# Two-direction state-space layer: another order for the last stage of each head group, the norm factor applied behind the last output products, and PSUM copies on ScalarE

## The reference, cut to what matters

```python
def ssd_mixer(u, w_in, conv_w, conv_b, dt_bias, a_log, d_skip, norm_w, w_out):
    proj = u @ w_in
    z = proj[..., :SSD_D_INNER]
    xbc = silu(dwconv_centred(proj[..., SSD_D_INNER:SSD_D_INNER + SSD_CONV_DIM], conv_w, conv_b))
    ...
    dt = softplus(dt_raw + dt_bias)
    y = y_fwd + y_bwd + xh * d_skip
    y = y * silu(z)
    yg = y.reshape(bsz, seq, SSD_GROUPS, SSD_D_INNER // SSD_GROUPS)
    yg = yg * rsqrt(mean(yg * yg, axis=-1, keepdims=True) + NORM_EPS)
    return (yg.reshape(bsz, seq, SSD_D_INNER) * norm_w) @ w_out
```

## Time and profile before

| | us |
|---|---|
| median of 3 runs | 1836.99 (1836.5 to 1837.8) |
| the profiled execution | 1833.54 |
| its span on the core | 1831.8 |
| PE busy in the span | 1578.1 (86%) |
| DVE busy | 1282.2 (70%) |
| ACT busy | 781.0 (43%) |
| POOL busy | 165.6 (9%) |

### The profile page before, as it was taken

How to read it: one execution, slowest core, us unless ns; L and a number is a source line. 1 busy time by engine, 2 the same in 40 slices (tenths; PEclk the granted TensorE clock), 3 DMA queues, 4 the chain that set the end, 5 groups by cost and what they waited for, 6 DMA issues and landing times.

```text
span 1831.8 us, 20798 instructions
## 1 busy us (share of the span) xinstructions
PE 1578.1 (86%) x7275; PEld 1269.4 (69%) x7275; DVE 1282.2 (70%) x1673; ACT 781.0 (43%) x1323; POOL 165.6 (9%) x200
## 2 busy tenths in 40 slices
PE   3984987987985799999998777887898999999996
PEld 1753756755754588778877556887686888888875
DVE  4577766866875676696679898997466677663355
ACT  3348465473473455513442322221234555542242
POOL 1153000000000450000001020000010000000000
PEclk7987998998997899999999986675899999999998
DMA  2233313303320523252334564662232323333231
GB/s 71 82 92 117 92 46 115 105 33 118 112 70 23 114 87 97 81 184 92 102 133 161 191 240 143 162 166 53 66 104 70 102 92 100 95 97 104 90 94 64
DMA packets 189607, 190.57 MB, mean 104 GB/s; under 512 B 47566, under 2 KB 178206, under 8 KB 185438
## 3 DMA queue, kind: packets, MB, share of 16 engines
q1 hardware_dynamic: 168926, 187.52, 32.4%
q10 hardware_dynamic: 20608, 2.10, 0.9%
HBM read 165.27 MB, written 24.31 MB: 103 GB/s over the span
## 4 chain that ended last, share of the span: by engine, by line
PE 59%; DVE 25%; ACT 9%; issue 4%; DMA 2%; ACTq 1%; SPq 1%; DVEq 0%
PE ring L1829 19%; PE ring L1830 18%; PE ring L1831 18%; ACT rows L992 3%; ACT rows L1002 3%; DVE w_lo L1224 2%; DVE rb L1631 2%; DMA rows<-log_decays 1%; DVE ul L1238 1%; PE pe_y L1972 1%; DVE cc L1348 1%; DVE s_prod L1590 1%; DVE tab L1551 1%; DVE ytmp L1502 1%; DVE rstd L1247 1%
## 5 line engine op out<-in xcount | busy, mean ns | idle before, releaser
L879 ACT ACTIVATE w_hi<-w_raw 128x1024 fp32r<-128x1024 f32 (+1 forms) x233 | 239.9, 1029 | 656.7 <-PE ring L1831 626.2
L1829 PE MATMUL ring<-uh,w_hi 128*128 128x512 f32 (+1 forms) x1160 | 461.9, 398 | 36.5 <-DVE w_lo L1224 30.1
L1830 PE MATMUL ring<-ul,w_hi 128*128 128x512 f32 (+1 forms) x1160 | 455.7, 393 | 0.0
L1831 PE MATMUL ring<-uh,w_lo 128*128 128x512 f32 (+1 forms) x1160 | 455.0, 392 | 0.0
L1224 DVE TENSOR_TENSOR w_lo<-w_raw,w_hi 128x1024 fp32r<-128x1024 f32 (+1 forms) x233 | 278.0, 1195 | 188.4 <-ACT w_hi L879 188.2
L1829 PEld LDWEIGHTS ring<-uh,w_hi 128*128 128x128 f32 (+1 forms) x1160 | 220.1, 190 | 94.7 <-DVE w_lo L1224 25.7
L1830 PEld LDWEIGHTS ring<-ul,w_hi 128*128 128x128 f32 (+1 forms) x1160 | 220.1, 190 | 47.3 <-issue 2.1
L1831 PEld LDWEIGHTS ring<-uh,w_lo 128*128 128x128 f32 (+1 forms) x1160 | 219.7, 189 | 47.4 <-issue 0.6
L1829 PE MATMUL ring<-gh,w_hi 128*128 128x512 f32 x480 | 190.5, 397 | 29.2 <-DVE w_lo L1224 16.1
L1830 PE MATMUL ring<-gl,w_hi 128*128 128x512 f32 x480 | 189.1, 394 | 0.0
L1831 PE MATMUL ring<-gh,w_lo 128*128 128x512 f32 x480 | 189.0, 394 | 0.0
(11 more groups left out here) (250 smaller groups left out, 2173.9 us busy)
## 6 DMA issues: line engine op xcount, KB each, us to landing
w_raw<-in_ffn_w_up SPq DMA_DIRECT2D x88, 512.0 KB, 3.5
w_raw<-in_ffn_w_down SPq DMA_DIRECT2D x40, 512.0 KB, 3.5
w_raw<-in_ssd_w_in SPq DMA_DIRECT2D x32, 512.0 KB, 4.4
rows<-log_decays SPq DMA_DIRECT2D x16, 1024.0 KB, 5.9
s_tables<-tab SPq DMA_DIRECT2D x16, 1024.0 KB, 6.2
slot<-s_tables SPq DMA_DIRECT2D x16, 1024.0 KB, 7.4
w_raw<-in_ssd_w_out SPq DMA_DIRECT2D x16, 512.0 KB, 3.5
w_raw<-in_ple_w_gate SPq DMA_DIRECT2D x16, 512.0 KB, 3.5
```

Of the source, the lines that this page charges most:

```text
L879: act.activation(w_hi[u % 2][:, 0:n], w_raw[:, u % 2, 0:n], ACT.Copy).then_inc(hi_done, 1)
L1829: pe.matmul(o, wh[:, k, c], rh[:, k0 + k, :], start=first and k == 0, stop=False)
L1830: pe.matmul(o, wh[:, k, c], rl[:, k0 + k, :], start=False, stop=False)
L1831: mm_ = pe.matmul(o, wl[:, k, c], rh[:, k0 + k, :], start=False, stop=last and k == nk - 1)
```

## The change

- ACT, not DVE, copies `xseq` (four tiles) and `bseq` out of PSUM, right behind the `hi` of the last z unit and ahead of the silu of z.
- PE, y stage: transposes of pairs 0 and 1 first; then per pair outputs, transposes two pairs ahead, and one filler product. In group 0 the fillers are the first two units of the next projection, behind pairs 1 and 3; in groups 1 and 2 the output products 1, 2, 3 of the group before behind pairs 0, 1, 2, and both projection units behind pair 3; in group 3 output products 1, 2 and 3 behind pairs 0, 1 and 3. `group_square` comes behind all that.
- DVE, y stage: add_yoff and weigh of pair 0; then per pair lo, take_out, finish, and add_yoff and weigh of the next pair.
- Last group: y is multiplied by the weight alone, per pair right behind its finish, rounded and its rest made per pair, into memory of its own (`yh_last`, `yl_last`). The norm factor `ytmp` multiplies the output products instead: `take_last_out` has two multiplications into a scratch tile and two additions to `h` where `take_out` had two additions. `group_square` of the last group stands behind its first output product.

```diff
@@ scalar
                 hi_to(z + 3)
+                for c in range(SB + 1):
+                    name, k = (("xseq", g), c) if c < SB else (("bseq", g), 0)
+                    act.wait_ge(evac, T[name] + k)
+                    act.wait_ge(filled, FILL[name] + k + 1)
+                    dst = xseq[:, c, :] if c < SB else bseq[:].rearrange("p c n -> p (c n)")
+                    act.activation(dst, bank(T[name] + k), ACT.Copy).then_inc(evac, 1)
...
+                def y_hi(m):
+                    act.wait_ge(yn_done, GT * g + m + 1)
+                    act.activation(YH[g][:, m, :], zs[:, m, :], ACT.Copy).then_inc(yh_done, 1)
                 for hp in range(GT + 1):
                     if hp + 2 < GT:
                         decays(hp + 2)
-                    if hp + 1 < GT and g:
+                    if g == GROUPS - 1:
+                        if hp:
+                            y_hi(hp - 1)
+                        if hp in (0, 2, 4):
+                            hi_to(w + 3 + hp // 2)
+                    elif hp + 1 < GT and g:
                         hi_to(w + hp + 3)
@@ vector
-                for c in range(SB):
-                    take(("xseq", g), c, xseq[:, c, :])
-                dve.wait_ge(filled, FILL[("bseq", g)] + 1)
-                dve.tensor_copy(bseq[:], bank(T[("bseq", g)]).rearrange("p (c n) -> p c n", c=SB)).then_inc(evac, 1)
+                dve.wait_ge(evac, T[("cb", g)])
...
+                add_yoff(0)
+                weigh(0)
                 for hp in range(GT):
-                    weigh(hp)
-                    if g:
-                        lo_to(w + hp + 2)
-                    add_yoff(hp)
-                    if hp:
-                        finish(hp - 1)
-                    if hp + 1 < GT and g:
-                        take_out(g - 1, hp + 1)
-                finish(GT - 1)
+                    if g and (g, hp) != (GROUPS - 1, 2):
+                        lo_to(w + hp + 2 - (g == GROUPS - 1 and hp == 3))
+                    if hp and g and (g, hp) != (GROUPS - 1, 3):
+                        take_out(g - 1, hp)
+                    finish(hp)
+                    if g == GROUPS - 1:
+                        dve.wait_ge(gated, GT * g + hp + 1)
+                        y_normed(hp, None)
+                    if hp + 1 < GT:
+                        add_yoff(hp + 1)
+                        weigh(hp + 1)
+                    if g == GROUPS - 1:
+                        y_rest(hp)
+                if g == GROUPS - 1:
+                    take_out(g - 1, 3)
+                    lo_to(w + 5)
...
+            def take_last_out(i):
+                t = T[("out", GROUPS - 1, i)]
+                part = rows_[0][:, 0].rearrange("p j l -> p (j l)").rearrange("p (j l) -> p j l", j=2)
+                dve.wait_ge(unit_done, U[("out", GROUPS - 1)] + i + 1)
+                if i:
+                    dve.wait_ge(evac, t)
+                for j in range(2):
+                    dve.tensor_tensor(part[:, j, :], bank(t + j), ytmp[:], ALU.mult).then_inc(out_scaled, 1)
+                for j in range(2):
+                    dve.wait_ge(out_scaled, 2 * i + j + 1)
+                    dve.wait_ge(evac, T[("out", GROUPS - 2, i)] + j + 1)
+                    dve.tensor_tensor(h[:, 2 * i + j, :], h[:, 2 * i + j, :], part[:, j, :], ALU.add).then_inc(evac, 1)
             for i in range(4):
-                take_out(GROUPS - 1, i)
+                take_last_out(i)
                 lo_to(U[("out", GROUPS - 1)] + i + 2)
@@ tensor
-                for i in range(3):
+                for i in range(g > 0, 3):
                     for kg in range(2):
-                        product(u + 2 * i + kg, ...)
-                        if g and (i, kg) == (0, 0):
-                            group_square(g - 1, GT - 1)
+                        xbc_product(g, i, kg)
...
+                after = ([None, ("xbc", 0), None, ("xbc", 1)],
+                         [("out", 1), ("out", 2), ("out", 3), ("xbc", 0), ("xbc", 1)],
+                         [("out", 1), ("out", 2), ("out", 3), ("xbc", 0), ("xbc", 1)],
+                         [("out", 1), ("out", 2), None, ("out", 3)])[g]
                 transposes(0)
+                transposes(1)
                 for hp in range(GT):
-                    if hp + 1 < GT and g:
-                        out_product(g - 1, hp + 1)
-                    if hp + 1 < GT:
-                        transposes(hp + 1)
                     outputs(hp)
-                    if hp:
-                        group_square(g, hp - 1)
-            group_square(GROUPS - 1, GT - 1)
+                    if hp + 2 < GT:
+                        transposes(hp + 2)
+                    meanwhile(after[hp])
+                for what in after[GT:]:
+                    meanwhile(what)
+                if g < GROUPS - 1:
+                    group_square(g, GT - 1)
             pe.wait_ge(yl_done, GT * GROUPS)
             for i in range(4):
                 out_product(GROUPS - 1, i)
+                if i == 0:
+                    group_square(GROUPS - 1, GT - 1)
```

More of the change, by code:

```diff
@@ L178, in bidir_hybrid_kernel @@
         zs = sb("zs", [P, GT, SEQ], where=ssd)
+        last_y = ExitStack()
+        yh_last = sb("yh_last", [P, GT, SEQ], F32R, last_y)
+        yl_last = sb("yl_last", [P, GT, SEQ], F32R, last_y)
+        last_y.close()
         xd = sb("xd", [P, 2, GC], where=ssd)
@@ L1025, in _ @@
                     hi_to(U[("xbc", g + 1)] + 2)
-                if g:
[L1027 to L1030, removed]
+                    if g:
+                        act.wait_ge(unit_done, w + 4)
+                    for m in range(GT):
+                        y_hi(m)
             for i in range(4):
@@ L1486, in _, with y_normed, y_rest @@
                         adds += 1
-                for hp in range(GT):
-                    weigh(hp)
-                    if g:
-                        lo_to(w + hp + 2)
-                    add_yoff(hp)
-                    if hp:
-                        finish(hp - 1)
-                    if hp + 1 < GT and g:
-                        take_out(g - 1, hp + 1)
-                finish(GT - 1)
+                def y_normed(m, factor):
+                    if factor is None:
+                        op = dve.tensor_scalar(zs[:, m, :], xT[:, m, :], col(C_SSDN + GT * g + m), None, ALU.mult)
+                    else:
+                        op = dve.scalar_tensor_tensor(out=zs[:, m, :], in0=xT[:, m, :], scalar=col(C_SSDN + GT * g + m),
+                                                      in1=factor, op0=ALU.mult, op1=ALU.mult)
+                    op.then_inc(yn_done, 1)
+                def y_rest(m):
+                    dve.wait_ge(yh_done, GT * g + m + 1)
+                    dve.tensor_tensor(YL[g][:, m, :], zs[:, m, :], YH[g][:, m, :].bitcast(F32), ALU.subtract
+                                      ).then_inc(yl_done, 1)
+                add_yoff(0)
+                weigh(0)
+                for hp in range(GT):
+                    if g and (g, hp) != (GROUPS - 1, 2):
[14 more added lines that the diff above has]
+                    lo_to(w + 5)
                 dve.wait_ge(gsq_used, 2 * g + 2)
@@ L1505, in _ @@
                     lo_to(U[("xbc", g + 1)] + 2)
[L1506 to L1513, removed]
+                    for m in range(GT):
+                        dve.wait_ge(gated, GT * g + m + 1)
+                        y_normed(m, ytmp[:])
+                    for m in range(GT):
+                        y_rest(m)
+            def take_last_out(i):
[10 more added lines that the diff above has]
+                    dve.tensor_tensor(h[:, 2 * i + j, :], h[:, 2 * i + j, :], part[:, j, :], ALU.add).then_inc(evac, 1)
             for i in range(4):
-                take_out(GROUPS - 1, i)
+                take_last_out(i)
                 lo_to(U[("out", GROUPS - 1)] + i + 2)
@@ L1903, in out_product, with xbc_product @@
                 def out_product(g, i):
-                    product(U[("out", g)] + i, T[("out", g, i)], GT, 0, yh, yl)
+                    product(U[("out", g)] + i, T[("out", g, i)], GT, 0, YH[g], YL[g])
+                def xbc_product(g, i, kg):
+                    product(U[("xbc", g)] + 2 * i + kg, T[("xbc", g)] + 2 * i, 4, 4 * kg, uh0, ul0, first=kg == 0,
+                            last=kg == 1)
                 u = U[("xbc", g)]
-                for i in range(3):
+                for i in range(g > 0, 3):
                     for kg in range(2):
-                        product(u + 2 * i + kg, T[("xbc", g)] + 2 * i, 4, 4 * kg, uh0, ul0, first=kg == 0, last=kg == 1)
-                        if g and (i, kg) == (0, 0):
-                            group_square(g - 1, GT - 1)
+                        xbc_product(g, i, kg)
                 z_product(0)
```

7 lines of the change are left out of this document (added).

## The result

The changed kernel takes 1855.57 us (median of 4 runs, 1854.70 to 1856.45), the kernel before 1837.39 (4 runs); the ratio is 1.0100 with a 95% interval of [1.0088, 1.0112]. The forecast was 1854.7. The profiled execution took 1856.45 us with a span of 1854.4, 22.6 longer than the span of before; the medians differ by 18.2.

The account below looks back on a forecast made before the run. PE was taken to set the pace, its y-stage waits for DVE hiding a wait for ACT. Group 0 +3.8, groups 1 and 2 +5.4 and last group +8.5 sum to +17.7 us: 1851.2 profiled, median 1854.7, 8-in-10 range 1841 to 1867.

Parts of the forecast that it names:

- Group 0, +3.8: Whole of group 0: softplus delay from the ACT copies plus a later y stage, +3.8 us (2.5 to 5).
- +3.2 of the copies: Group 0: copies ahead of silus, table load and softplus steps on ACT delay DVE and PE by 3.2 us.
- I find it 0.6 us later: Group 0's y stage: outputs of the last pair come 0.6 us later, behind outputs 2, finish, add_yoff and weigh.
- Groups 1 and 2, +5.4: Y stage of groups 1 and 2: +3.8 less 1.1 for copies, +2.7 each (0.8 to 4.8), +5.4 together.
- Copies in groups 1 to 3, -1.1 each: Groups 1 to 3: ACT copies remove PE's 1.1 us wait, -1.1 us per group; other end 0.
- Last group, +8.5: Last group: later y stage and slower tail, +9.6 less 1.1 for copies, +8.5 us (4 to 14).
- my steps (531.6 to 579.4): Last group's y stage: product 1, decays, DVE queue and outputs summed from 531.6 to last outputs ending at 579.4.
- the 580 below which the prediction would have been wrong: Last group: the prediction counts as wrong if the last products start before 580; the sum put them at 586.4.
- (1): Rival: fillers carry the y stage and ACT is never last; -17 us, 1820 us; chance 0.11.
- (2): Rival: the last group gains its norm wait, paying for the other three; about +-3 us, 1837 us; chance 0.08.
- (3): Rival: worse tail from DVE meeting POOL and PE at 1.2 GHz, steps 8.5 instead of 6.5; 1870 us; chance 0.1.
- up to 7.6 us of POOL in the tail: Tail: by the exclusive-lock rule six POOL additions of 1.27 could cost DVE up to 7.6 us; not in the sum.

Follow-up runs that it names:

- r3: Changed kernel with the rests of y in the last group made one pair later; 1843.97 us, ratio 1.0050 to the kernel before.
- r6: Changed kernel without the multiplications by the last group's norm factor in the last steps; 1850.04 us, ratio 1.0062 to the kernel before.
- r8: Kernel before with only the copies moved to ACT, in groups 1 to 3; 1836.43 against 1837.52 us, ratio 0.9995.
- r5: Kernel before with only the copies moved to ACT, in all groups; 1839.19 us, ratio 1.0013.
- r2: Changed kernel with the squares of groups 0 to 2 between the projection units, group 0's first unit behind pair 3; 1848.64 us, ratio 1.0070.
- r9: Kernel before's order, ACT copies in groups 1 to 3, last group's factor behind its products, rests late, squares ahead of products; 1830.88 us, ratio 0.9966.
- r1: Changed kernel with the copies of xseq and bseq back on DVE in group 0 only; 1848.52 us, ratio 1.0073 to the kernel before.
- r0: Changed kernel run once more without any edit, as measure for other runs; 1853.87 against 1835.18 us for the kernel before, ratio 1.0101.
- r11: Changed kernel with fourteen useless matmuls in PE's wait ahead of the first outputs of groups 1 and 2; 1856.74 us, ratio 1.0106.

## Why the prediction was right, and where its terms were not

**Group 0, +3.8; +5.7 and +5.5 measured.** The +3.2 of the copies came as forecast: X to Y rose by 3.3 (47.4 to 50.7), and the row named for it stands at

```profile
124.54 2.08 PE L1928 MATMUL ring<-ad_seq,tri 128*128 128x128 f32 x8 [3.76 <-DVE ad_seq L1326]
```

2.05 later than in the earlier trace rows, in an execution that reached the group 1.2 us earlier. The step at "I find it 0.6 us later" is the mis-sized term, 2.5 instead of 0.6 (Y to V). Three things are in it. The last weigh meets POOL twice, where in before it met it once:

```profile
176.65 2.17 DVE L1396 TENSOR_TENSOR rows<-rows 128x1024 f32<-128x1024 f32 x1
```

```profile
176.48 1.26 POOL L700 TENSOR_TENSOR var<-sq 128x512 f32<-128x512 f32 x1 [22.67 <-ACT sq L1021]
```

That is 1.1 more, and I had no meeting in group 0. E to V took 8.8 instead of 7.8, at a granted clock of 0.84 instead of 0.94. The last 0.4 is what is left for the order itself.

**Groups 1 and 2, +5.4; +3.5 measured.** Each link is there: PE idle 4 us behind the first two transposes,

```profile
282.28 1.09 PE L2024 MATMUL pe_y<-rows,xseq 128*64 128x128 f32 x4 [4.01 <-DVE rows L1413]
```

ACT's `hi` behind an output product, and 6.09 us in front of `w_lo`. The group's period came to 132.9 in group 1 (132 forecast), but to 129.9 in group 2. The sum put Y to V at 50.3 and its gain over before at +3.8. Two terms of it were mis-sized. One is the base: I read group 1 alone, whose y stage in before took 46.4 from Y to V, while the one of group 2 took 48.1. The other is the new stage, which took 51.1 or 48.0; which of the two goes with the granted clock between Y and E, 0.83 and 0.90, and not with the group (r3, r6). With both groups of before read, group 2 would have stood at +1.0 and the two at +3.7. That this is near the measured +3.5 is luck: in group 2 the stage came 2.3 us shorter than the sum and the copies 1.3 us dearer.

**Copies in groups 1 to 3, -1.1 each: a third of it by r8's median.** The wait of the earlier trace rows went, but in group 2 the time came back as chunk states at the low clock (3.3 us in after, 3.5 in r5, 3.7 in r8, for 2.3). I had allowed 0 as the other end and taken the upper one without a reason in the rows.

**Last group, +8.5; +12.7 and +10.3 measured.** DVE was idle 12.5 in front of y_rest (11 forecast), and PE in front of the third and fourth outputs:

```profile
576.74 2.85 PE L2024 MATMUL pe_y<-rows,xseq 128*64 128x128 f32 x16 [13.63 <-DVE rows L1413]
...
586.97 2.85 PE L2024 MATMUL pe_y<-rows,xseq 128*64 128x128 f32 x16 [7.37 <-DVE rows L1413]
```

Y to E was 49.8 where my steps (531.6 to 579.4) give 47.8; 2.0 of it are again two meetings, at DVE instructions of 2.17 (574.43) and 2.28 (583.28) us, of which the sum had 0.4. The first last product and the factor took what was forecast: 603.78 to 608.56 is 4.8. The tail took 26.2 for 24.9, since two of three steps came near 6.9 and not 6.5. X to Y came at +0.2 where the copies were to bring -1.1. The last products started at 596.4, well behind the 580 below which the prediction would have been wrong. r3 shows that the stall is the cause and not a symptom: without it the last group is back at 82.1.

**The total.** The forecast was 1854.7 and the median 1855.6; that it lies so near is in part luck. The four terms missed by +1.9, +0.7, -2.6 and +4.2, and the profiled executions stand 22.6 apart where the medians stand 18.2 apart.

**Rivals.** The fillers do not carry the stage (1): DVE still waits for `w_hi` in it, 3.1 and 2.4 us in group 1. But they do shorten it up to the last outputs: Y to E took 38.0 and 35.2 in groups 1 and 2, before 38.4 and 40.1. What was won there was lost from E to V, 13.1 and 12.9 instead of 8.0, since both projection units stood ahead of the squares; r2 moves the squares and shows it. No gain in the last group paid for the others (2), though r3 and r9 show that it was to be had. For (3), DVE's steps did pass 5.75 and PE did wait, but with steps up to 6.9 and not 8.5. The estimate of up to 7.6 us of POOL in the tail counts six additions; the trace of before has five there, which add six squares.

## What to carry over

Finishing an item "at once" moves every instruction of its chain to the head of a queue in which other work waits: before doing so, look on the feeding engine for what stands ahead of the input, and leave one item of distance if it isn't ready (here one DVE instruction one pair later was worth 9.9 us). Filler work belongs beside a latency chain, not ahead of the instruction that starts it: the same new order was slower than the old one in groups 1 and 2 with both units ahead of the squares, and faster with one behind them. And where a loop has several like passes, read all of them before taking one as the base; here they differed by 1.7 us, half of the effect.

## What the runs showed of the chip

**In these runs VectorE and GpSimd took turns where both operands of VectorE's instruction are in SBUF.** Five DVE instructions of 128x1024 that began while a POOL addition of 128x512 ran took 2.17 to 2.29 us instead of 1.22: 0.95 to 1.07 more, which is the remainder of the addition less 0.14 or so (DVE from 177.11 beside POOL until 178.20 in r1). A DVE instruction already running isn't lengthened; then POOL's own grows, from 1.27 up to 2.31. An addition with one operand in PSUM was not lengthened: `take_out` of group 1 in after ran its two in 1.27 us, as always, while POOL added from 314.08 to 315.49.

```profile
314.29 1.27 DVE L1389 TENSOR_TENSOR h<-h,ring 128x512 f32<-128x512 f32 x2
```

The Trainium skill, "SBUF — State Buffer", section "Who interferes with whom", says that a VectorE instruction with two SBUF inputs contends with a GpSimd one that reads SBUF, over a port pair that is an exclusive lock. The trace agrees. That a meeting cost less than the full 1.27, which the prediction read as lying below the rule, comes from when it began: part of the addition was over already. The prediction had put such a meeting at half of 0.75.

**A won or lost microsecond is partly given back by the clock.** 1.2 GHz spells followed PE's waits (outputs behind a wait of 4.0 us took 2.85 us, others 1.58), moved with the edits and between executions of the same code, and made like stages differ by 3.1 us (51.1 and 48.0). Gains of one microsecond (r8) and of eleven (r2) both arrived only in part. The clock of group 1's y stage was 0.83 in r0, 0.90 in r3 and r6 without any edit there, and 0.96 in r11, whose time did not fall. What decides where a spell begins and ends stays open.
